# The last block's turning: eight units through the matrix engine, or through 32x32 blocks and memory

## The chip, the cores and the metric

One core of a Trainium2 chip runs the whole program. The metric is the device time of one execution in microseconds (us), lower is better. Engines are named as in the profile: PE is TensorE (PEld its weight loads), DVE VectorE, ACT ScalarE, POOL GpSimd, SP the queue that issues most transfers.

## The reference, cut to what matters

Two blocks of a network on 256 tokens of width 1024; the change lies in the second one, whose mixer is this (one layer, 16 heads of 64):

```python
proj = jnp.einsum("bsd,dc->bsc", h, w_in)                 # 1024 -> 10240 columns
xc, bg, cg, zc, q, k, v, za, g_conv, g_attn = jnp.split(proj, splits, axis=-1)
c = causal_depthwise_conv(cg * xc, conv_w)                # three taps along the tokens
y_conv = jnp.einsum("bsc,cd->bsd", jax.nn.silu(zc) * bg * c, w_out_conv)
o = mixture_of_dilations(q, k, v, slopes)                 # softmax attention, three patterns
y_attn = jnp.einsum("bsc,cd->bsd", jax.nn.silu(za) * o, w_out_attn)
merged = sigmoid(g_conv + b) * y_conv + sigmoid(g_attn + b) * y_attn
return jnp.einsum("bsd,de->bse", merged, w_o)
```

## The kernel before, in words

Tokens lie on partitions in two tiles of 128. All weights pass through a ring: SP loads a slot of 1 MB (two transfers of 512 KB, `load`, L483 to L500) into one of three raw buffers, ACT rounds it to the high part (`round_hi`, L675), POOL subtracts for the low part in four pieces (`subtract`, L642), and PE multiplies with high and low parts (`across_tile`, L2062, L2063, L2065: 24 matmuls of 512 columns for both token tiles). SP asks for the low part of the slot three back before it loads the next, ACT rounds four slots ahead of PE (`ahead`), and the split buffers are six.

`HI` is the input product of the last block: 40 slots, two for each of 20 column groups of 512, in the order q, q, k, k, v, v, then the inputs of the convolution (6 to 9), gates (10 to 15) and merge gates (16 to 19). Each engine's `hybrid` walks through the same loop over groups `c` and halves `j` and does its share of the other work between slots. From `c = 5` on, one `step(k)` per slot handles the heads: PE makes scores of two heads at each even step (L2604) and the value products of head k - 5 (L2620 to L2622); DVE adds the position bias (L1767), takes maxima (L1769, L1770), and for head k - 1 multiplies with the pattern table and sums (L1775, L1777) and turns the probabilities by 32x32 blocks (`v.transpose`, L1783); ACT exponentiates (L1104).

Two ways of turning stand side by side. The probabilities go through memory: after DVE's block transposes of a pair of heads, SP stores them in four transfers (L556), waits for these, and loads them in four more, in pieces of 128 bytes, to their turned place (L562); `turn_heads(m)` does this after the weight load of slot 19 + 2m. The other eight units, q (two), k (two), the convolution's input (7, 9) and the convolution's gate (11, 13), are turned by PE: `unit` (L2624) makes four transposes per token tile into one PSUM bank, and ACT copies them to SBUF (`units`, L1114); for 11 and 13 DVE multiplies them out of PSUM (`z_units`, L1831). The convolution itself (`convolve`, L1819 to L1821) is DVE's, eight pieces of 128 channels, three passes each.

The turned probabilities are the stationary operand of the value products, q that of the scores, k the moving operand of the scores. Waits are explicit semaphores, and each engine executes its instructions in the order written.

Of the kernel before, what the change touches and what calls it, by code (L numbers as in the profile page):

```python
# [23 lines left out]
F32 = mybir.dt.float32  # L24
F32R = mybir.dt.float32r
# [6 lines left out]
P = 128  # L32
# [107 lines left out]
def program(nc, A, out):  # L140
    ctx = ExitStack()
    with ctx:
# [14 lines left out]
        pT_hi = sb("pT_hi", [P, 2, TILES * P], F32R)  # L157
        pT_lo = sb("pT_lo", [P, 2, TILES * P], F32R)
# [3 lines left out]
        causal = sb("causal", [P, LCOLS])  # L162
        upto = sb("upto", [P, P])
        ones = sb("ones", [P, P])
        last_row = sb("last_row", [P, P])
# [16 lines left out]
        def area(at, *shape):  # L182
# [5 lines left out]
            if len(shape) == 3:  # L188
# [61 lines left out]
        h_bounce = [nc.dram_tensor(f"h_bounce{w}", (4, P, 2 * LCOLS // 4), F32, kind="Internal").ap()  # L250
# [10 lines left out]
        H_UNITS = {0: h_qT[:, 0:4], 1: h_qT[:, 4:8], 2: h_kT[:, 0:4], 3: h_kT[:, 4:8], 7: h_uT[:, 0:4],  # L261
                   9: h_uT[:, 4:8], 11: None, 13: None}
# [183 lines left out]
        h_pl_in_psum = sem("h_pl_in_psum")  # L446
        h_pl_ready = sem("h_pl_ready")
# [23 lines left out]
        def _(sp):  # L471
# [93 lines left out]
            def linear(s0, w, cols, halves_first=False, after={}):  # L565
# [5 lines left out]
                for i, (col, j) in enumerate(order):  # L571
# [4 lines left out]
                    if i in after:  # L576
                        turn_heads(after[i])

            def ple(name, w_proj, w_gate):
# [19 lines left out]
            linear(S["HI"], A["w_in_2"][0], [512 * c for c in H_ORDER],  # L599
                   after={H_TURN_SLOT + 2 * m: m for m in range(AH // 2)})  # L600
# [12 lines left out]
        def _(pool):  # L613
# [8 lines left out]
            pool.memset(causal[:], 0.0).then_inc(consts_ready, 1)  # L622
            pool.memset(upto[:], 1.0).then_inc(consts_ready, 1)
            pool.memset(ones[:], 1.0).then_inc(consts_ready, 1)
            pool.memset(last_row[:], 0.0).then_inc(consts_ready, 1)
# [6 lines left out]
            pool.affine_select(out=upto[:], in_=upto[:], compare_op=ALU.is_ge, fill=0.0, base=0,  # L632
                               pattern=[[1, P]], channel_multiplier=-1).then_inc(consts_ready, 1)
            pool.affine_select(out=last_row[:], in_=last_row[:], compare_op=ALU.not_equal, fill=1.0,
# [27 lines left out]
        def _(act):  # L662
# [214 lines left out]
            def p_hi(layer):  # L877
                act.wait_ge(pt_in_psum, layer + 1)
                nc.scalar.copy(pT_hi[:], (acc[:, 1, 0:512], tb[:, 1, :])[layer].rearrange("p (k c) -> p k c", k=2)
                               ).then_inc(pt_hi_ready, 1)  # L880
# [209 lines left out]
            def hybrid():  # L1090
# [17 lines left out]
                def units(c):  # L1108

                    dst = H_UNITS[c]  # L1110
# [1634 lines left out]
```

## Time and profile before

| | |
|---|---|
| median of 3 runs | 1367.21 us (1365.07 to 1367.71) |
| profiled execution | 1366.17 us, span 1364.4 us |
| granted clock of PE in it | 0.997 of full speed |
| busy in the span | PE 1348.8, PEld 1121.2, DVE 624.0, ACT 658.0, POOL 1140.3 us |
| moved by DMA | 255.36 MB, mean 187 GB/s |

The page gives busy times of the engines; matmul ends are modelled, so the spacing of starts tells more than the busy share. Windows give the same by stretch of time; the lists of waits tell which instruction stood idle for which other; the order of time shows single instructions. The input product of the last block takes the stretch from about 1040 to 1288 us, its middle 32 slots from 1063 to 1266.

### The profile page before, as it was taken

The numbers are of one execution on the slowest core, as the hardware profiler recorded it, in microseconds if no ns is written. First come the engines' busy times: TensorE is split into PE (matmuls) and PEld (weight loads), VectorE is DVE, ScalarE is ACT, GpSimd is POOL, SyncE is SP. The second block draws the span as 40 slices with busy tenths as digits, with TensorE's granted clock in tenths as the row PEclk, the third lists the DMA queues.
The fourth block names the chain that finished last, engine by engine and source line by source line (L and its number), as shares of the span: only waits on it lengthen the run. The fifth ranks groups of instructions, "written<-read, shape, count | busy, mean of one in ns | idle before, by whom it ended". The sixth has DMA issues, their size and how long they took to land.

```text
span 1364.4 us, 19630 instructions
## 1 busy us (share of the span) xinstructions
PE 1348.8 (99%) x6723; PEld 1121.2 (82%) x6723; DVE 624.0 (46%) x1570; ACT 658.0 (48%) x757; POOL 1140.3 (84%) x913
## 2 busy tenths in 40 slices
PE   8999999999999999999999999999999999999997
PEld 6888888888888888888888778888888888878886
DVE  6233344654333356623333885333346236862224
ACT  6444454546444456444443676444446443444431
POOL 5999977849999969999998539999978977779882
PEclk9999999999999999999999999999999999999999
DMA  8666654536666555766558426665545557767540
GB/s 273 215 201 208 206 183 144 185 106 225 197 192 194 194 171 171 237 210 211 184 184 217 139 77 208 210 198 187 184 154 196 192 193 202 215 183 256 190 165 31
DMA packets 199488, 255.36 MB, mean 187 GB/s; under 512 B 42844, under 2 KB 137860, under 8 KB 199300
## 3 DMA queue, kind: packets, MB, share of 16 engines
q1 hardware_dynamic: 197140, 247.82, 57.0%
q10 hardware_dynamic: 2288, 6.75, 1.4%
q8 instruction: 37, 0.61, 0.2%
q14 instruction: 23, 0.19, 0.0%
HBM read 249.29 MB, written 5.24 MB: 187 GB/s over the span
## 4 chain that ended last, share of the span: by engine, by line
PE 92%; DVE 4%; ACT 1%; DMA 1%; issue 1%; SPq 0%; ACTq 0%; DVEq 0%
PE tb L2152 9%; PE gu L2152 9%; PE acc L2062 8%; PE acc L2063 8%; PE acc L2065 7%; PE acc L2099 6%; PE acc L2102 6%; PE acc L2107 6%; PE gu L2062 5%; PE gu L2063 5%; PE tb L2158 4%; PE gu L2158 4%; PE gu L2065 3%; PE gu L2070 2%; PE tb L2065 1%; PE tb L2062 1%
## 5 line engine op out<-in xcount | busy, mean ns | idle before, releaser
L642 POOL TENSOR_TENSOR w_lo<-w_raw,w_hi 128x512 fp32r<-128x512 f32 x896 | 1135.3, 1315 | 197.1 <-ACT w_hi L675 193.7
L675 ACT CAST w_hi<-w_raw 128x2048 fp32r<-128x2048 f32 x225 | 427.8, 1909 | 146.1 <-DMA w_raw<-in_w_ffn_in 36.3
L2152 PE MATMUL gu<-xT,w_hi 128*128 128x512 f32 x512 | 202.3, 395 | 0.0
L2152 PE MATMUL tb<-xT,w_hi 128*128 128x512 f32 x512 | 202.2, 395 | 0.0
L2062 PE MATMUL acc<-w_hi,xT 128*128 128x512 f32 x496 | 198.3, 400 | 0.0
L2063 PE MATMUL acc<-w_lo,xT 128*128 128x512 f32 x496 | 193.1, 389 | 0.0
L2065 PE MATMUL acc<-w_hi,xT 128*128 128x512 f32 x468 | 182.7, 390 | 0.0
L1378 DVE TENSOR_TENSOR arena<-gu,arena 128x256 f32<-128x256 f32 x64 | 27.2, 425 | 300.5 <-PE gu L2152 300.5
L2158 PE MATMUL tb<-xT,w_lo 128*128 128x256 f32 x512 | 140.4, 280 | 0.0
L2158 PE MATMUL gu<-xT,w_lo 128*128 128x256 f32 x512 | 139.8, 279 | 0.0
L2062 PE MATMUL gu<-w_hi,xT 128*128 128x512 f32 x312 | 123.4, 395 | 1.1 <-ACT xT L720 1.1
L2063 PE MATMUL gu<-w_lo,xT 128*128 128x512 f32 x312 | 121.4, 389 | 0.0
L2158 PEld LDWEIGHTS tb<-xT,w_lo 128*128 128x128 f32 x512 | 96.4, 188 | 20.2
L2158 PEld LDWEIGHTS gu<-xT,w_lo 128*128 128x128 f32 x512 | 96.2, 188 | 19.1
L2062 PEld LDWEIGHTS acc<-w_hi,xT 128*128 128x128 f32 x496 | 93.2, 188 | 18.9 <-issue 1.2
L2063 PEld LDWEIGHTS acc<-w_lo,xT 128*128 128x128 f32 x496 | 93.3, 188 | 18.2 <-issue 0.2
L2099 PE MATMUL acc<-w_hi,hidden_T 128*128 128x512 f32 x336 | 104.4, 392 | 0.0
L2102 PE MATMUL acc<-w_lo,hidden_T 128*128 128x512 f32 x336 | 103.6, 390 | 0.0
L2107 PE MATMUL acc<-w_hi,hidden_T 128*128 128x512 f32 x336 | 103.5, 389 | 0.0
L2065 PEld LDWEIGHTS acc<-w_hi,xT 128*128 128x128 f32 x468 | 87.8, 188 | 18.9
L866 ACT ACTIVATE arena<-gu 128x256 f32<-128x256 f32 x32 | 12.3, 384 | 182.0 <-DVE gu L1381 182.0
L2152 PEld LDWEIGHTS tb<-xT,w_hi 128*128 128x128 f32 x512 | 97.1, 190 | 2.6
(364 smaller groups left out, 1969.0 us busy)
## 6 DMA issues: line engine op xcount, KB each, us to landing
w_raw<-in_w_ffn_in SPq DMA_DIRECT2D x176, 512.0 KB, 4.7
w_raw<-in_w_ffn_out SPq DMA_DIRECT2D x88, 512.0 KB, 4.1
w_raw<-in_w_in SPq DMA_DIRECT2D x80, 512.0 KB, 4.6
w_raw<-in_mlstm_w_in SPq DMA_DIRECT2D x24, 512.0 KB, 4.3
w_raw<-in_w_ple_gate SPq DMA_DIRECT2D x16, 512.0 KB, 4.1
w_raw<-in_w_kv SPq DMA_DIRECT2D x16, 512.0 KB, 4.3
w_raw<-in_mlstm_w_out SPq DMA_DIRECT2D x8, 512.0 KB, 4.5
w_raw<-in_diff_w_q SPq DMA_DIRECT2D x8, 512.0 KB, 5.2
```

The costliest lines, as they stand in the source:

```text
L642: ins = pool.tensor_tensor(w_lo[:, slot.spl, cols], w_raw[:, slot.raw, cols], w_hi[:, slot.spl, cols].bitcast(F32), ALU.subtract)
L675: nc.scalar.copy(w_hi[:, slot.spl, :], w_raw[:, slot.raw, :]).then_inc(hi_ready, 1)
L1378: v.tensor_tensor(part, low, rs_row, ALU.mult).then_inc(row_step, 1)
L2062: mm(out, xh, wh, start=(half == 0 and k == 0), stop=False)
L2063: mm(out, xh, wl, start=False, stop=False)
L2065: last = mm(out, xl, wh, start=False, stop=(half == 1 and k == 3))
L2070: last = mm(out, xl, wh, start=False, stop=(half == 1 and k == 3))
L2099: mm(acc[:, t, 512 * half:512 * half + 512], a_hi[:, k, tok(t)], w(w_hi, half), start=st, stop=False)
L2102: mm(acc[:, t, 512 * half:512 * half + 512], a_hi[:, k, tok(t)], w(w_lo, half), start=False, stop=False)
L2107: last = mm(acc[:, t, 512 * half:512 * half + 512], a_lo[:, k, tok(t)], w(w_hi, half), start=False, stop=sp_)
L2152: return mm(pair_of(j), w_hi[:, slot.spl, at:at + P], xT[:, 4 * half + k, :, :].rearrange("p a c -> p (a c)"), start=(half == 0 and k == 0 ...
L2158: return mm(pair_of(j)[:, 0:2 * P], w_lo[:, slot.spl, at:at + P], xT_hi[:, 4 * half + k, :], start=False, stop=False)
```

## The change

PE's transposes of the eight units, ACT's copies and the PSUM bank between them go. DVE turns each unit by 32x32 blocks right behind its evacuation (`turn_unit`), SP stores it to memory in four transfers that put the blocks to their turned partitions, and loads it back in one. q and k come back as before (channel block, then token). The convolution's input and gate come back token by token, with the four channel blocks side by side (a step of 16 bytes from token to token); the probabilities likewise with their six blocks (a step of 24 bytes from query to query), in one transfer of 3 KB per partition in place of four with pieces of 128 bytes. A second buffer of blocks for the heads is laid over tables that are no longer used. Storing and loading of a pair of heads stand behind the weight loads of different slots. The convolution's pieces come one to two slots later, its gate is multiplied at groups 15 and 17 in one pass over both token tiles, and the merge bias is loaded in two halves.

```diff
-H_CONVOLVE = {(9, 0): 0, (9, 1): 1, (10, 0): 2, (10, 1): 3, (11, 0): 4, (12, 0): 5, (12, 1): 6, (13, 0): 7}
-H_UNITS_AT = {(2, 0): 0, (2, 1): 1, (3, 0): 2, (4, 0): 3, (8, 1): 7, (10, 1): 9, (12, 1): 11, (14, 1): 13}
+H_CONVOLVE = {(10, 0): 0, (10, 1): 1, (11, 0): 2, (11, 1): 3, (13, 0): 4, (13, 1): 5, (14, 0): 6, (14, 1): 7}
+H_GATE_AT = {(15, 0): 11, (17, 0): 13}
+H_UNITS = (0, 1, 2, 3, 7, 9, 11, 13)
+H_BLOCKS_FREE = {7: 3, 9: 7, 11: 0, 13: 11}
+H_STORE_UNITS = {10: (0, 1), 12: (2,), 14: (3,), 22: (7,), 27: (9,), 31: (11,), 34: (13,)}
+H_LOAD_UNITS = {11: (0, 1), 13: (2,), 15: (3,), 23: (7,), 28: (9,), 32: (11,), 35: (13,)}
...
-        h_uT = area(8192, 8, 256)
+        h_uT = area(8192, 2, 256, 4)
-        h_pb = area(13056, 4, 2 * 3 * 32)
+        h_pb = [area(13056, 4, 2 * 3 * 32), tables[:].rearrange("p a b -> p (a b)").rearrange("p (j n) -> p j n", j=4)]
-            "p (w i n) -> p w i n", w=2, i=6)
+            "p (w c n) -> p w c n", w=2, n=6)
...
-            def turn_heads(m):
+            def scatter_blocks(bounce, blocks, stored):
+                pieces = bounce.rearrange("(b j) (n i a) -> b (j n) i a", j=4, i=4, a=32)
+                for i in range(4):
+                    sp.dma_start(pieces[:, :, i, :],
+                                 blocks[32 * i:32 * i + 32].rearrange("b j (n a) -> b (j n) a", a=32)
+                                 ).then_inc(stored, 16)
+            def scatter_runs(bounce, blocks, n, stored):
+                pieces = bounce.rearrange("(b j) (t i r) -> b (j t) i r", j=4, i=4, r=32 * n)
...
+            def store_heads(m):
                 sp.wait_ge(h_blocks_turned, 2 * m + 2)
-                if m:
-                    sp.wait_ge(h_pt_landed, 64 * m)
-                for i in range(4):
-                    sp.dma_start(h_bounce[m % 2][i].rearrange("(j b) n -> b j n", j=4), h_pb[32 * i:32 * i + 32]
-                                 ).then_inc(h_bounced, 16)
+                scatter_runs(h_bounce[m % 2], h_pb[m % 2], 6, h_bounced)
+            def load_heads(m):
                 if m >= 2:
                     sp.wait_ge(h_pv_in_psum, 2 * m - 2)
+                if m:
+                    sp.wait_ge(h_pt_landed, 16 * m)
                 sp.wait_ge(h_bounced, 64 * (m + 1))
-                for i in range(4):
-                    sp.dma_start(h_pT[:, m % 2, :, 32 * i:32 * i + 32],
-                                 h_bounce[m % 2][i].rearrange("c (n a) -> c n a", a=32)).then_inc(h_pt_landed, 16)
+                sp.dma_start(h_pT[:, m % 2].rearrange("p c n -> p (c n)"), h_bounce[m % 2]).then_inc(h_pt_landed, 16)
+            def store_unit(c):
+                sp.wait_ge(h_unit_turned, H_UNIT_NO[c] + 2)
...
+            def load_unit(c):
+                n = H_UNITS.index(c)
+                sp.wait_ge(h_unit_stored, 128 if n < 2 else 64 * (n + 1))
+                if n:
+                    sp.wait_ge(h_unit_landed, 16 * n)
+                sp.dma_start(h_turned[c].rearrange("p k c -> p (k c)"), h_unit_bounce[c]).then_inc(h_unit_landed, 16)
+            def turns_after(i):
+                m = i - H_TURN_SLOT
+                if m >= 0 and m % 2 == 0 and m // 2 < AH // 2:
+                    store_heads(m // 2)
+                if m >= 1 and m % 2 == 1 and m // 2 < AH // 2 - 1:
+                    load_heads(m // 2)
+                if m == AH - 2:
+                    load_heads(AH // 2 - 1)
+                for c in H_LOAD_UNITS.get(i, ()):
+                    load_unit(c)
+                for c in H_STORE_UNITS.get(i, ()):
+                    store_unit(c)
...
-                        if h >= 2 and h % 2 == 0:
-                            dve.wait_ge(h_bounced, 64 * (h // 2))
-                        to = h_pb[:, :, 96 * (h % 2):96 * (h % 2) + 96].rearrange("p j (n a) -> p n j a", n=3)
-                        v.transpose(to, s.rearrange("p (n j b) -> p n j b", n=3, j=4)).then_inc(h_blocks_turned, 1)
+                        if h >= 4 and h % 2 == 0:
+                            dve.wait_ge(h_bounced, 64 * (h // 2 - 1))
+                        to = h_pb[(h // 2) % 2].rearrange("p j (a n) -> p n j a", n=6)[:, 3 * (h % 2):3 * (h % 2) + 3]
+                        v.transpose(to, s.rearrange("p (n b j) -> p n j b", n=3, j=4)).then_inc(h_blocks_turned, 1)
...
+                def turn_unit(c):
+                    if c in H_BLOCKS_FREE:
+                        dve.wait_ge(h_unit_stored, 64 * (H_UNITS.index(H_BLOCKS_FREE[c]) + 1))
+                    for t in range(TILES):
+                        dve.wait_ge(h_evac, H_EVAC[c] - 1 + t)
+                        if c < 4:
+                            to = h_blocks[c].rearrange("p j (k t a) -> p t k j a", t=TILES, a=32)[:, t]
+                        else:
+                            to = h_blocks[c].rearrange("p j (t a k) -> p t k j a", t=TILES, a=32)[:, t]
+                        v.transpose(to, h_s[:, H_PLACE[c], t, :].rearrange("p (k b j) -> p k j b", j=4, b=32)
+                                    ).then_inc(h_unit_turned, 1)
...
+                    z = h_zT[:, 4 * half:4 * half + 4, :]
+                    v.tensor_tensor(z, h_turned[c].rearrange("p c k -> p k c"), z, ALU.mult).then_inc(h_z_ready, 2)
...
-                            return h_pT[:, (h // 2) % 2, 3 * (h % 2) + n, :]
+                            return h_pT[:, (h // 2) % 2, :, 3 * (h % 2) + n]
...
-                def unit(c, t):
-                    pe.wait_ge(h_evac, H_EVAC[c])
...
-                    for k in range(4):
-                        ins = nc.tensor.transpose(tb[:, 1, tok(k)], h_s[:, H_PLACE[c], t, tok(k)], ident[:])
-                    ins.then_inc(h_pl_in_psum, 1)
```

## Rows read from the trace of the kernel before

**Rows 1.** The page, part 1: busy us (share of span) and instructions by engine.

```profile
PE 1348.8 (99%) x6723; PEld 1121.2 (82%) x6723; DVE 624.0 (46%) x1570; ACT 658.0 (48%) x757; POOL 1140.3 (84%) x913
```

**Rows 2.** Windows: busy us of PE, PEld, DVE, ACT, POOL; clock, DMA share, GB/s.

```profile
1157.00:1184.00 27.00, 26.78 (x138) 21.76 (x136) 21.82 (x54) 14.12 (x18) 17.15 (x15) 1.00 0.74 214
1184.00:1206.00 22.00, 21.29 (x112) 16.81 (x110) 19.15 (x39) 8.90 (x10) 19.29 (x15) 1.00 0.75 217
```

**Rows 3.** All waits of PE, 1063 to 1266 us: total, times, longest.

```profile
PE tb L2634 <- DVE arena L1831: 0.9, 1, 0.9
PE tb L2634 <- ACT arena L1114: 0.2, 1, 0.2
```

**Rows 4.** PE in order of time around one unit's transposes: start, duration.

```profile
1065.62 0.39 PE L2063 MATMUL acc<-w_lo,xT 128*128 128x512 f32 x1
1065.85 0.39 PE L2065 MATMUL acc<-w_hi,xT 128*128 128x512 f32 x1
1066.08 0.60 PE L2634 MATMUL tb<-ident,arena 128*128 128x128 f32 x4
1066.43 0.47 PE L2062 MATMUL acc<-w_hi,xT 128*128 128x512 f32 x1
1066.74 0.39 PE L2063 MATMUL acc<-w_lo,xT 128*128 128x512 f32 x1
```

**Rows 5.** PE in order of time around the transposes that waited longest.

```profile
1204.90 0.39 PE L2065 MATMUL acc<-w_hi,xT 128*128 128x512 f32 x1
1206.19 0.63 PE L2634 MATMUL tb<-ident,arena 128*128 128x128 f32 x4 [0.90 <-DVE arena L1831]
```

**Rows 6.** PE in order of time around the first value product.

```profile
1135.40 0.39 PE L2065 MATMUL acc<-w_hi,xT 128*128 128x512 f32 x1
...
1135.63 0.33 PE L2620 MATMUL gu<-arena,hidden_T 128*128 128x64 f32 x2
...
1136.21 0.48 PE L2062 MATMUL acc<-w_hi,xT 128*128 128x512 f32 x1
```

**Rows 7.** Groups of instructions, 1063 to 1266 us: busy, mean ns | idle before, releaser.

```profile
L642 POOL TENSOR_TENSOR w_lo<-w_raw,w_hi 128x512 fp32r<-128x512 f32 x133 | 170.7, 1324 | 34.4 <-ACT w_hi L675 34.4
...
L2634 PE MATMUL tb<-ident,arena 128*128 128x128 f32 x64 | 9.6, 272 | 1.1 <-DVE arena L1831 0.9 <-ACT arena L1114 0.2
L1783 DVE STREAM_TRANSPOSE arena<-arena 128x384 f32<-128x384 f32 x16 | 9.1, 567 | 15.0 <-DMA h_bounce<-arena 15.0
```

**Rows 8.** DVE, then POOL, in order of time, 1158 to 1170 us.

```profile
1158.43 0.42 DVE L1777 CUSTOM_DVE_ANT_0 arena<-arena,times 128x256 f32<-128x256 f32 x1
...
1162.40 1.50 DVE L1777 CUSTOM_DVE_ANT_0 arena<-arena,times 128x256 f32<-128x256 f32 x1
...
1161.02 9.06 POOL L642 TENSOR_TENSOR w_lo<-w_raw,w_hi 128x512 fp32r<-128x512 f32 x7 [2.74 <-ACT w_hi L675]
```

**Rows 9.** Groups of DVE's instructions, 540 to 580 us (another stage).

```profile
L1986 DVE TENSOR_TENSOR arena<-arena,gcol 128x1024 f32<-128x1024 f32 x2 | 4.6, 2325 | 0.0
...
L1979 DVE STREAM_TRANSPOSE arena<-arena 128x1024 f32<-128x1024 f32 x2 | 2.4, 1224 | 0.0
```

**Rows 10.** PE, POOL and SP's queue in order of time: the first pair.

```profile
1117.22 0.93 PE L2604 MATMUL gu<-arena 64*128 64x128 f32 x8
...
1122.11 10.27 POOL L642 TENSOR_TENSOR w_lo<-w_raw,w_hi 128x512 fp32r<-128x512 f32 x8 [1.92 <-ACT w_hi L675]
...
1126.73 2.63 SPq L562 DMA_DIRECT2D hidden_T<-h_bounce  x4
```

**Rows 11.** Transfers issued from 1063 to 1266 us: KB each, median us to landing.

```profile
w_raw<-in_w_in SPq DMA_DIRECT2D x62, 512.0 KB, 4.6
h_bounce<-arena SPq DMA_DIRECT2D x32, 96.0 KB, 4.3
hidden_T<-h_bounce SPq DMA_DIRECT2D x32, 96.0 KB, 2.8
...
arena<-in_b_merge ACTq DMA_DIRECT2D x1, 1024.0 KB, 4.5
```

More of the change, by code:

```diff
@@ L161, in program @@
         ident = sb("ident", [P, P])
[L162 to L165, printed above, removed]
+        tables = sb("tables", [P, 6, P])
+        causal = tables[:, 0:3].rearrange("p a b -> p (a b)")
+        upto, ones, last_row = (tables[:, i] for i in (3, 4, 5))
         gcol = sb("gcol", [P, 168])
@@ new lines, in scatter_runs @@
+            def scatter_runs(bounce, blocks, n, stored):
+                pieces = bounce.rearrange("(b j) (t i r) -> b (j t) i r", j=4, i=4, r=32 * n)
+                for i in range(4):
+                    sp.dma_start(pieces[:, :, i, :],
+                                 blocks[32 * i:32 * i + 32].rearrange("b j (t r) -> b (j t) r", r=32 * n)
+                                 ).then_inc(stored, 16)
+            def store_heads(m):
+                sp.wait_ge(h_blocks_turned, 2 * m + 2)
+                scatter_runs(h_bounce[m % 2], h_pb[m % 2], 6, h_bounced)
@@ L567, in linear @@
+            def linear(s0, w, cols, halves_first=False, after=None):
                 src = w.rearrange("(k p) c -> p k c", p=P)
@@ L575, in linear @@
                                  src[:, 4 * j + 2 * k:4 * j + 2 * k + 2, col:col + 512]) for k in range(2)])
-                    if i in after:
-                        turn_heads(after[i])
+                    if after:
+                        after(i)
             def ple(name, w_proj, w_gate):
@@ L598, in _ @@
             ple("P1", A["w_ple_proj"][1], A["w_ple_gate"][1])
-            linear(S["HI"], A["w_in_2"][0], [512 * c for c in H_ORDER],
-                   after={H_TURN_SLOT + 2 * m: m for m in range(AH // 2)})
+            linear(S["HI"], A["w_in_2"][0], [512 * c for c in H_ORDER], after=turns_after)
             linear(S["HC"], A["w_out_conv_2"][0], both)
@@ L878, in p_hi @@
                 act.wait_ge(pt_in_psum, layer + 1)
-                nc.scalar.copy(pT_hi[:], (acc[:, 1, 0:512], tb[:, 1, :])[layer].rearrange("p (k c) -> p k c", k=2)
+                nc.scalar.copy(pT_hi, (acc[:, 1, 0:512], tb[:, 1, :])[layer].rearrange("p (k c) -> p k c", k=2)
                                ).then_inc(pt_hi_ready, 1)
@@ L1106, in step @@
                         ins.then_inc(h_exped, 1)
-                def units(c):
-                    dst = H_UNITS[c]
-                    for t in range(TILES):
-                        w = H_UNIT_NO[c] + t
-                        act.wait_ge(h_pl_in_psum, w + 1)
-                        nc.scalar.copy(dst[:, :, tok(t)], tb[:, 1, :].rearrange("p (k c) -> p k c", k=4)
-                                       ).then_inc(h_pl_ready, 1)
                 steps = 0
@@ L1121, in hybrid @@
                             ahead(At(s0 + 2 * c + j))
-                        if H_UNITS.get(H_UNITS_AT.get((c, j))) is not None:
-                            units(H_UNITS_AT[c, j])
                         if c >= 5 and steps < H_STEPS:
@@ L1822, in convolve, with gate_conv @@
                                            ).then_inc(h_conv, 1)
-                def z_units(c):
+                def gate_conv(c):
                     half = (c - 11) // 2
                     dve.wait_ge(h_conv, 4 * half + 4)
-                    for t in range(TILES):
-                        dve.wait_ge(h_pl_in_psum, H_UNIT_NO[c] + t + 1)
-                        z = h_zT[:, 4 * half:4 * half + 4, tok(t)]
-                        v.tensor_tensor(z, tb[:, 1, :].rearrange("p (k c) -> p k c", k=4), z, ALU.mult
-                                        ).then_inc(h_z_ready, 1)
+                    dve.wait_ge(h_unit_landed, 16 * (H_UNITS.index(c) + 1))
+                    z = h_zT[:, 4 * half:4 * half + 4, :]
+                    v.tensor_tensor(z, h_turned[c].rearrange("p c k -> p k c"), z, ALU.mult).then_inc(h_z_ready, 2)
                 def gate_before_sigmoid(c, t):
-                    dve.wait_ge(h_bm_landed, 16)
+                    dve.wait_ge(h_bm_landed, 16 if c < 18 else 32)
                     dve.wait_ge((tile0_used, slot_used)[t], s0 + 2 * c + 2)
                     g = (h_gc, h_ga)[c // 18][:, t, 512 * (c % 2):512 * (c % 2) + 512]
-                    v.scalar_tensor_tensor(g, bank(c, t), r(t), h_bm[:, 512 * (c - 16):512 * (c - 16) + 512],
+                    v.scalar_tensor_tensor(g, bank(c, t), r(t), h_bm[:, 512 * ((c - 14) % 4):512 * ((c - 14) % 4) + 512],
                                            ALU.mult, ALU.add).then_inc(h_gpre, 1)
@@ L1844, in hybrid @@
                     for j in range(2):
-                        if H_UNITS_AT.get((c, j)) in (11, 13):
-                            z_units(c - 1)
                         if c >= 5 and steps < H_STEPS:
@@ L2329, in cumulate @@
                     pe.wait_ge(m_logf, 1)
-                    mm(tb[:, 1, 16:24], upto[:], m_lf, start=True, stop=True).then_inc(m_cum, 1)
+                    mm(tb[:, 1, 16:24], upto, m_lf, start=True, stop=True).then_inc(m_cum, 1)
                 chunk(2, {0: turn_gates, 3: cumulate})
@@ L2337, in spread @@
                         pe.wait_ge(m_am_ready, t)
[L2338 removed]
+                    mm(tb[:, 0, :], ones, m_diag, start=True, stop=True).then_inc(m_spread, 1)
                 chunk(3, {0: lambda: spread(0)})
                 pe.wait_ge(m_last_rhs, 1)
[L2343 removed]
+                mm(tb[:, 1, 24:32], last_row, m_last, start=True, stop=True).then_inc(m_last_in_psum, 1)
                 spread(1)
@@ L2647, in hybrid @@
                             across_tile(At(s0 + 2 * c + j), j, t, acc_outs(c % 2, t))
-                            if (c, j) in H_UNITS_AT:
-                                unit(H_UNITS_AT[c, j], t)
                         if c >= 5 and steps < H_STEPS:
```

72 lines of the change are left out of this document (42 added, 30 removed).

## The prediction

> **What bounds the kernel now.** I read the page's busy times first: TensorE (PE) is busy 1348.8 of 1364.4 us [rows 1]. A busy PE row cannot tell a full engine from one that stretches, so I went on to the windows of the stage that the change touches, the 40 weight slots of the last block's input product, about 1063 to 1266 us. In its two densest windows PE is busy in 26.78 of 27 and 22.00 of 22 us, VectorE (DVE) in 21.82 and 19.15, GpSimd (POOL) in 17.15 and 19.29, ScalarE (ACT) in 14.12 and 8.90 [rows 2]. PE is the bound, DVE is second. PE's own waits in the whole stage come to 1.1 us, both in front of the transposes that the change removes, one for DVE's gate product and one for ACT's copy [rows 3]. The third view is the order of time on PE: matmuls of 512 columns follow each other every 0.23 us (1065.62, 1065.85) [rows 4]. A slot is 24 of them, 5.5 us, and whatever else stands in PE's queue is added to the end of the kernel.
>
> **What is removed from PE.** Eight units of two token tiles are turned by PE, four transposes each, 64 in all [rows 7]. From the last matmul before such a four (1065.85) to the first behind it (1066.43) it is 0.58 us, and that first one takes 0.31 to the next: over two beats of 0.23 that is 0.43 us [rows 4]. I take 0.44, and 16 x 0.44 = **7.0 us** go. With them go the two waits. One is seen directly: the last matmul starts at 1204.90 and the transposes at 1206.19, 1.29 us for a beat of 0.23 [rows 5], so 1.06; the other is 0.2 [rows 3]. Together **1.3 us**. Nothing moves in between to take their place at once, since the next work in the queue, values of a head or the next slot, asks for things that are ready. PE's sum is -8.3 us.
>
> **What is added to PE.** No instruction. But the 48 value products now load their probabilities with 24 bytes between neighbouring columns (six blocks side by side) instead of 4. Before, a head's six loads and products take 1135.40 to 1136.21, 0.81 us less a beat, plus the 0.08 behind: 0.66, or 0.11 us a pass [rows 6]. The product has only 64 columns, so the pass is paced by its weight load of 128 columns, and a slower load is seen in full. No load in the trace has such a step. Bounds: 0, or a load of twice the time, 96 x 0.11 = 10.6 us. I take 0: the load draws 128 columns in 0.11 us, 0.86 ns each, whereas the same memory feeds moving columns at 0.23 us for 512, 0.45 ns each [rows 4, 6], so the load asks for half the pace that is proven. That is an argument for spare speed in contiguous order, not a measurement of steps, and the upper end stays in the range.
>
> The Trainium skill speaks against this layout: Advanced Engine Details and Errata, section SBUF Cachelines, says that SBUF lines are 16 bytes, that two hits on a line are needed to absorb the memory's latency, and that a new line at each access costs. By it each column at 24 bytes is a new line and the 10.6 us would come. It gives no size, and no row of the trace of before has such an access. It is the first rival below.
>
> **What is added to DVE.** 16 transposes of 128x512. The key transposes elsewhere in the kernel take 1.224 us for 128x1024 and the head transposes 0.567 for 128x384 [rows 7, 9], so 0.61 to 0.76 each, 10 to 12 us in all. The four gate products of 0.69 from PSUM become two of 128x1024 out of SBUF, 2.325 us each by the nearest row [rows 9], +1.9. What goes is DVE's wait for the bounce buffer, 15.0 us [rows 7], because it is doubled. Transposes, convolution and gate also get steps of 16 and 24 bytes; as above 0, upper end a doubling (16 x 0.57 for the heads, 16 x 0.6 for the units, some 0.5 for each of 24 convolution passes: 31 us, spread over 150). All of this lies beside PE's slots. The cover is this: at each step PE's value product waits for the row maxima of a head whose scores were issued a slot, 5.5 us and more, earlier. DVE's cost of a step depends on POOL: the same 128x256 pass takes 0.42 us when POOL is idle and 1.50 when it works (POOL is idle for 2.74 us up to 1161.02 and busy behind it) [rows 8]. With POOL working, I make a step 4.2 us and a convolution 3.5. The four slots of the convolutions 0 to 3 then ask 31 us of DVE with their 2.9 us of evacuation and unit transposes, against 4 x 6.6 on PE with its head work. It falls 5 us behind, which is just the cover. I charge 1.0 us.
>
> **What moves on the queues.** SP issued 64 transfers for the heads; now it issues 40 for them and 40 for the units, between the same weight loads. Where it waits, weight loads wait behind it, then ACT's rounding and POOL's subtraction. POOL finishes slots 17 and 18 at 1132.4, so slot 17 about 1127.3, while PE, which ends slot 15 at 1135.6, cannot reach it before 1141.7 [rows 6, 10]: a lead of 14 us. A unit holds SP for four issues (about 0.45 each), a store (4.3) and a load's issue [rows 11], some 7 us. The lead covers that; without it the loss would be 7 us less what is left. Bytes: the 8 units add 0.5 MB out and in each; of pieces of 128 bytes 16,400 come (units 0 to 3, 128 x 32 each) and 24,600 go (8 pairs, 128 x 24). Weights land in 4.6 us now [rows 11], and 2 us more on some of them is covered as well. Units 0 to 2 are needed at the end of slot 10, unit 2 is evacuated after slot 5, 27 us before, and its own chain (DVE 2.7, store 4.3 to 9, load 4.6) takes 12 to 16: nothing.
>
> The new wait that could tell is the probabilities'. SP used to stay for the bounce and to load the pair at once; now the load goes behind the next slot's weights, which wait for POOL's low part three slots back. For the first pair: scores start at 1117.22 and end at 1118.1, POOL has slot 17 at 1127.3, then two weight issues (0.9) and the pair's load, between 2.8 on its own and 4.6 + 2.8 one after the other [rows 10, 11]: 1131 to 1135.6. PE asks at 1135.6 [rows 6]. Later pairs have about 2 us more, for value products then stand between. Before, the same load was issued at 1126.73 [rows 10]. So a stall of 0 to 1 us for the first and little for others; with a DVE that is behind, its lag adds to this chain. I charge 0.5 us.
>
> **ACT and POOL.** ACT loses 12 copies, with the waits in front of them. It is not the bound, so 0; its rounding comes a little earlier, which helps the chain above. The merge bias is loaded in two halves; the second is issued behind ACT's sigmoids of slot 35 and lands some 4.5 us later [rows 11]. DVE asks for it after slot 37's first tile, and PE then still has six half slots, 6 x 12 x 0.23 = 16.6 us, before it needs what DVE makes of it: 0. POOL: 33 slots of 4 x 1.324 are 171 us of 203 [rows 7]; with 195 it still fits.
>
> **Sum**, against the profiled execution's 1366.17 us (span 1364.4): -7.0 - 1.3 + 1.0 + 0.5 = -6.8, 1359.4. The median of the runs shown, 1367.21, stands 1.0 above that execution; I predict **1359.6**.
>
> **The rivals.**
> (a) *The strided weight loads are slow.* Place: the 96 loads of the value products. Price up to +10.6; it decides from a pass of 0.20 us on, because then 96 x 0.09 eats the 8.3. At twice the time, with 1.5 for DVE and the queue, 1366.2 - 8.3 + 10.6 + 1.5 = 1370.0, **slower**; DVE's passes at half speed would add stalls and make it 1372. For it: the layout is new to the trace, and the pass is paced by the load. Against: the spare pace above. Chance 0.25.
> (b) *The wait moves to the probabilities.* DVE falls behind and the pair's load lies behind weights, so PE stalls at most of the 8 pairs by 0.5 to 1 us beyond my 1.5. For it: DVE is busy 41 of 49 us in the dense windows [rows 2], and the slack of 0 to 4 us is worked out from single landings. Against: 15.0 us of waiting leave DVE [rows 7], and SP no longer stays for the bounce. Time 1362 to 1367, say 1364.5. Chance 0.2.
> (c) *The time does not change because something else paces PE.* If POOL's 5.3 us a slot ruled, PE's removed work would turn into waits for low parts. Against: POOL idles 34.4 us in the stage for want of ACT's rounding [rows 7], and PE never waits for it [rows 3]. Time 1366. Chance 0.05.
> My forecast, 0.5: 1357.5 to 1361.5.
>
> **How the numbers follow.** About 0.2%, 2.7 us, is what a measurement of this kernel can tell from no change, so faster means below 1364.5, slower above 1369.9. Faster: 0.5 and half of (b), 0.1, with a little of (a) where the loads are only half as slow again (1364): 0.62. Slower: two thirds of (a), 0.17. The rest is the same, 0.21. The range starts at 1357.0, all of 8.3 gained with a run 1 us below the profiled one, and reaches over (b) and (c) into (a) to 1370.0, with about 0.15 beyond it.
>
> **What would show it.** In the profile after, no transposes between the matmuls of this stage: the spacing is 0.23 throughout with gaps only at scores and values. The six passes of a value product span 0.58 us over a beat as before; 1.2 would be (a). PE's waits: if the load of the probabilities from the bounce, or DVE's maxima, stand in front of PE with over 4 us in total, it is (b); waits for low parts would be (c). DVE's unit transposes take 0.6 to 0.8 us; if 1.2, steps cost DVE. The prediction is wrong if the end comes less than 4 us earlier, or if more than 9 us go, which no row of PE's queue could supply.

## The result, and the profile after

The change makes the kernel slower: 1372.47 us in the median (1370.88 to 1373.20) against 1367.23 us before (1365.07 to 1367.88), a ratio of 1.0039 with a 95% interval of [1.0029, 1.0048]. A seventh execution took 1917.47 us at a granted clock of 0.654 and is left out of the range and the ratio. The profiled execution took 1372.22 us, its span is 1370.5 us; before they were 1366.17 and 1364.4.

PE's transposes of units are gone from the stage and its busy time rose all the same. The page of the changed kernel, part 1, answers to [rows 1]:

```profile
PE 1352.1 (99%) x6659; PEld 1125.6 (82%) x6659; DVE 658.5 (48%) x1584; ACT 651.6 (48%) x745; POOL 1146.7 (84%) x913
```

64 instructions fewer and 3.3 us more: something on PE got longer. The order of time on PE shows what. First a value product that waits for nothing, the counterpart of [rows 6]:

```profile
1151.97 0.40 PE L2126 MATMUL acc<-w_hi,xT 128*128 128x512 f32 x1
1152.21 0.44 PE L2683 MATMUL gu<-arena,hidden_T 128*128 128x64 f32 x2
1152.49 0.61 PE L2684 MATMUL gu<-arena,hidden_T 128*128 128x64 f32 x2
1152.93 0.61 PE L2685 MATMUL gu<-arena,hidden_T 128*128 128x64 f32 x2
1153.35 0.47 PE L2123 MATMUL acc<-w_hi,xT 128*128 128x512 f32 x1
```

From the last matmul before it to the first behind it are 1.38 us, before 0.81 [rows 6]. Two passes are 0.44 us apart (1152.49, 1152.93): 0.22 us a pass, twice the 0.11 of before. That is 0.57 us a head, for 16 heads 9.1 us, more than the 8.3 that the prediction takes off PE.

The second loss stands at the first pair of heads, in the order of time on PE of the changed kernel:

```profile
1131.67 0.39 PE L2126 MATMUL acc<-w_hi,xT 128*128 128x512 f32 x1
1134.91 0.71 PE L2683 MATMUL gu<-arena,hidden_T 128*128 128x64 f32 x2 [2.85 <-DMA hidden_T<-h_bounce]
1135.41 0.65 PE L2684 MATMUL gu<-arena,hidden_T 128*128 128x64 f32 x2
1135.86 0.65 PE L2685 MATMUL gu<-arena,hidden_T 128*128 128x64 f32 x2
1136.27 0.77 PE L2123 MATMUL acc<-w_hi,xT 128*128 128x512 f32 x1
...
1141.54 0.46 PE L2123 MATMUL acc<-w_hi,xT 128*128 128x512 f32 x1
```

PE starts 3.24 us after the last matmul, 3.0 more than a beat, because the probabilities are not there. Behind the wait the next 12 matmuls take 5.27 us (1136.27 to 1141.54), where 12 beats of 0.227 are 2.72: another 2.55 us. The windows of the changed kernel say why (columns as in [rows 2]):

```profile
1131.00:1136.30 5.30, 2.45 (x12) 1.95 (x10) 4.20 (x10) 2.70 (x3) 5.30 (x5) 0.86 0.78 265
1136.30:1141.50 5.20, 5.20 (x13) 4.08 (x14) 3.68 (x5) 0.00 (x0) 5.20 (x5) 0.50 0.90 282
1157.00:1184.00 27.00, 27.00 (x129) 22.39 (x128) 20.62 (x48) 10.54 (x14) 18.43 (x15) 1.00 0.74 224
```

PE stood idle for 2.85 us, and then the granted clock is 0.50, the 1.2 GHz level, for the whole next window; PE counts as busy all the while. Later the clock is full again, and PE has no gap.

Why the probabilities are late is seen in SP's queue of the changed kernel (start, time over which the issues of one line go on, count):

```profile
1069.13 8.37 SPq L565 DMA_DIRECT2D h_unit<-arena  x8
...
1080.00 6.00 SPq L605 DMA_DIRECT2D arena<-h_unit  x2
1086.05 0.94 SPq L510 DMA_DIRECT2D w_raw<-in_w_in  x2
1087.04 6.11 SPq L565 DMA_DIRECT2D h_unit<-arena  x4
...
1097.48 7.20 SPq L565 DMA_DIRECT2D h_unit<-arena  x4
...
1124.75 2.72 SPq L573 DMA_DIRECT2D h_bounce<-arena  x4
...
1130.16 0.34 SPq L589 DMA_DIRECT2D hidden_T<-h_bounce  x1
```

The stores of units 0 to 3 go out in pieces of 128 bytes, and four such transfers hold SP for 4 to 7 us (L565). The loads of the first two units hold it as well (1080.00, 6.00 us): the second is issued only when the first has landed, and SP stands for 5.3 us of that time. What SP issues after them, the weights and then the pair's blocks, is late, and the pair is loaded at 1130.16 against 1126.73 before [rows 10]. Meanwhile PE is early: its first value product could have started at 1131.9, not at the 1135.6 of before [rows 6].

DVE and POOL do more. Groups of the changed kernel, 1063 to 1272 us, against [rows 7, 9]:

```profile
L697 POOL TENSOR_TENSOR w_lo<-w_raw,w_hi 128x512 fp32r<-128x512 f32 x131 | 175.1, 1374 | 35.8 <-ACT w_hi L730 35.8
L1851 DVE STREAM_TRANSPOSE arena<-arena 128x512 f32<-128x512 f32 x14 | 14.8, 1102 | 0.0
...
L1831 DVE STREAM_TRANSPOSE tables<-arena 128x384 f32<-128x384 f32 x8 | 7.5, 937 | 0.0
```

DVE's wait for the bounce buffer (15.0 us) is gone, the unit transposes take 1.10 us, those of the heads 0.93 where they took 0.567. PE waits for neither DVE nor POOL: all its waits in the changed kernel, 1063 to 1272 us (total, times, longest; [rows 3] before), are

```profile
PE gu L2683 <- DMA hidden_T<-h_bounce: 2.8, 1, 2.8
```

The account against the span of before: value products +9.1, wait for the first pair +3.0, low clock +2.55, together +14.7; the span grew by 6.1, so the removed transposes and their waits gave 8.6. That is a remainder, but it can also be read directly. Where four transposes stood in [rows 4], between 1065.85 and 1066.43, the order of time on PE of the changed kernel now has

```profile
1065.78 0.39 PE L2126 MATMUL acc<-w_hi,xT 128*128 128x512 f32 x1
1066.00 0.39 PE L2123 MATMUL acc<-w_hi,xT 128*128 128x512 f32 x1
```

The 16 such places, compared matmul by matmul in the two profiles, give 8.5 us: 0.45 at each, and 1.3 of waits. Ahead of the stage and behind it the two kernels run alike, to within 0.1 us.

### The profile page after: what moved, and what is told of

It reads as the page before. It is cut to its first block, busy times and chain, and to the rows that moved or that the text cites. A ratio compares the mean times of both kernels' runs of the same rounds, so it can differ in the third digit from the quotient of the medians.

```text
span 1370.5 us, 19512 instructions
## 1 busy us (share of the span) xinstructions
PE 1352.1 (99%) x6659; PEld 1125.6 (82%) x6659; DVE 658.5 (48%) x1584; ACT 651.6 (48%) x745; POOL 1146.7 (84%) x913
## 4 chain that ended last, share of the span: by engine, by line
POOL 62%; issue 18%; PE 17%; DMA 2%; DVE 1%; ACT 0%; SPq 0%; POOLq 0%; ACTq 0%; DVEq 0%
POOL w_lo L697 62%; PE acc L2123 4%; PE acc L2126 4%; PE acc L2124 4%; DMA w_raw<-in_w_ffn_in 1%; PE tb L2126 1%; PE tb L2124 1%; PE tb L2123 1%; PE gu L2126 1%; PE gu L2123 1%; PE gu L2124 1%; PE gu L2684 1%; PE gu L2685 1%; PE gu L2683 0%; DMA hidden_T<-h_bounce 0%
## 5 line engine op out<-in xcount | busy, mean ns | idle before, releaser
L2213 PEld LDWEIGHTS gu<-xT,w_hi 128*128 128x128 f32 x512 | 96.3, 188 | 2.8 <-DVE hidden_T L1444 0.4
```

What stands on the lines that cost most here:

```text
L2213: return mm(pair_of(j), w_hi[:, slot.spl, at:at + P], xT[:, 4 * half + k, :, :].rearrange("p a c -> p (a c)"), start=(half == 0 and k == 0 ...
```

## The experiments

**1. The store a slot earlier.** The change with the heads' blocks stored and loaded one slot earlier.

```diff
-H_TURN_SLOT = 19
+H_TURN_SLOT = 18
```

> The changed kernel with one number changed: each pair of heads is stored behind the weights of the slot before (18 + 2m in place of 19 + 2m) and loaded behind 19 + 2m. Theory: of the 14 to 15 us that the change adds, 9.5 are value products whose passes take 0.22 us in place of 0.11, and 5.8 are one event, PE's 3.2 us of waiting for the first pair and the 2.6 us that half the clock costs behind it; 8.6 go with PE's transposes. Then the wait and the low clock go here, the passes stay at 0.22, and the time is 1366.5 (1365 to 1368). Rival, the stall is the new pace of SP's queue and comes back at a later pair: 1370 to 1373. Rival, the half clock has nothing to do with the stall: PE still runs some 6.8 us at 0.5 somewhere in this stage, 1369.

Measured 1367.15 us, ratio 1.0001 [0.9992, 1.0010]. All waits of PE in this kernel, 1063 to 1266 us (total, times, longest):

```profile
PE gu L2667 <- DMA arena<-h_unit: 0.6, 1, 0.6
```

No wait for the pair is left, the clock stays at 1.00 through the stage, the passes stay at 0.22. The wait and the low clock cost 5.3 us (1372.47 - 1367.15), close to the 3.0 + 2.55 of the account; without them the change moves nothing, for about 9 us went and 9 us came.

**2. Packed probabilities.** The change with the probabilities in packed blocks as before (four transfers in, four out), at the places of the change.

```diff
-            "p (w c n) -> p w c n", w=2, n=6)
+            "p (w i n) -> p w i n", w=2, i=6)
...
-                            return h_pT[:, (h // 2) % 2, :, 3 * (h % 2) + n]
+                            return h_pT[:, (h // 2) % 2, 3 * (h % 2) + n, :]
```

> The changed kernel with the heads' part alone undone: probabilities packed again (128 neighbouring columns, loaded in four transfers in pieces of 128 bytes), stored and loaded behind the same slots as in the change; the eight units stay with DVE and memory. Theory, the 24-byte step of the stationary operand doubles its load: the six passes are back at 0.11 us each, the stall of the first pair and the half clock behind it stay or shrink, and the time is 1363 (1359 to 1364). Rival, the passes are slow for another reason (transfers that run at the same time, more of them than before): they stay at 0.2 and the time stays at 1372.

Measured 1368.82 us, ratio 1.0018 [1.0008, 1.0028]: 5 to 6 us above what was expected. The passes did go back to 0.11. The order of time on PE in this kernel, at the first pair, shows the miss:

```profile
1132.15 0.39 PE L2130 MATMUL acc<-w_hi,xT 128*128 128x512 f32 x1
1137.04 0.69 PE L2687 MATMUL gu<-arena,hidden_T 128*128 128x64 f32 x2 [4.50 <-DMA hidden_T<-h_bounce]
1137.52 0.63 PE L2688 MATMUL gu<-arena,hidden_T 128*128 128x64 f32 x2
1137.95 0.63 PE L2689 MATMUL gu<-arena,hidden_T 128*128 128x64 f32 x2
```

The wait grew to 4.7 us over a beat instead of staying at 3.0, and two later pairs waited as well (6.9 us in three waits). At the first pair PE asks no sooner than in the changed kernel (1132.15 against 1131.67). What is longer is the issue of the load: four transfers in pieces of 128 bytes take 3.89 us from 1130.54 on, one transfer took 0.34 us at 1130.16. The granted clock then falls to 0.50 here too. Curing one loss made the other larger: the two parts have to be undone together.

**3. Both.** Packed probabilities and the store a slot earlier.

> Both at once: packed probabilities and the store one slot earlier. Theory: 1367.2 - 8.6 = 1358.6, at best 1357, with no wait of PE over 0.5 us from slot 4 to 36 and no low clock; faster than both kernels. Rival, DVE or SP's queue holds PE up once it is faster: 1361 to 1366, with waits of PE for maxima, for probabilities or for low parts.

Median 1362.88 us, ratio 0.9982 [0.9966, 0.9998], but the 12 times lie in two groups: eight from 1360.72 to 1363.85 and four from 1369.27 to 1371.37. The profiled execution, 1369.79, belongs to the upper group. No value product waits in it. The lower group lies 2 to 5 us above the 1358.6 that was expected, in the range of the rival, and the profile has a wait of its kind: 1.9 us for a low part of POOL's in the last slots. The larger loss is in three orders of time of this kernel, of PE, DVE and POOL:

```profile
1281.93 0.39 PE L2130 MATMUL acc<-w_hi,xT 128*128 128x512 f32 x1
1288.93 0.76 PE L2127 MATMUL gu<-w_hi,xT 128*128 128x512 f32 x1 [6.61 <-DVE xT L1937]
...
1275.14 14.24 DVE L1937 TENSOR_TENSOR xT<-arena,xT 128x512 fp32r<-128x512 f32 x2
...
1290.63 1.28 DVE L1937 TENSOR_TENSOR xT<-arena,xT 128x512 fp32r<-128x512 f32 x2
...
1254.63 33.61 POOL L701 TENSOR_TENSOR w_lo<-w_raw,w_hi 128x512 fp32r<-128x512 f32 x27
```

Two subtractions of DVE that take 1.28 us a little later took 14.24 us. POOL worked from 1254.63 to 1288.24 without a pause, and DVE was through at 1289.38. PE, which needs these low parts for the next projection, lost 6.8 us, and its granted clock was 0.50 for the next 5 us, which cost some 2.5 more. The two groups are about 8.4 us apart.

**4. The step by itself.** The stationary operand of the value products is read at steps of 1, 2, 3, 4, 5 and 6 columns, by heads; the store is a slot earlier, and other probabilities than the reference's are multiplied.

```diff
+                            g = (1, 1, 1, 2, 2, 2, 3, 3, 3, 4, 4, 4, 5, 5, 6, 6)[h]
```

> The store one slot earlier, and the stationary operand of the value products is read with another step in each group of heads, from the same landed buffer: 1 column for heads 0 to 2, 2 for 3 to 5, 3 for 6 to 8, 4 for 9 to 11, 5 for 12 and 13, 6 for 14 and 15 (4, 8, 12, 16, 20, 24 bytes). It multiplies with wrong probabilities. One profile gives the pass for each step. Theory by 16-byte lines that want two hits: 0.11 us at 4 and 8 bytes, something between at 12, 0.22 from 16 on. Rival, any step but 4 bytes doubles the load: 0.22 from 8 on. Rival, it is not the step: the same at all.

The order of time on PE in this kernel; two rows a head, two passes apart, at steps of 4, 8, 12, 16 and 24 bytes:

```profile
1132.85 0.39 PE L2686 MATMUL gu<-arena,hidden_T 128*128 128x64 f32 x2
1133.07 0.39 PE L2687 MATMUL gu<-arena,hidden_T 128*128 128x64 f32 x2
...
1159.62 0.40 PE L2686 MATMUL gu<-arena,hidden_T 128*128 128x64 f32 x2
1159.85 0.40 PE L2687 MATMUL gu<-arena,hidden_T 128*128 128x64 f32 x2
...
1173.11 0.51 PE L2686 MATMUL gu<-arena,hidden_T 128*128 128x64 f32 x2
1173.45 0.51 PE L2687 MATMUL gu<-arena,hidden_T 128*128 128x64 f32 x2
...
1201.56 0.63 PE L2686 MATMUL gu<-arena,hidden_T 128*128 128x64 f32 x2
1202.02 0.63 PE L2687 MATMUL gu<-arena,hidden_T 128*128 128x64 f32 x2
...
1228.50 0.61 PE L2686 MATMUL gu<-arena,hidden_T 128*128 128x64 f32 x2
1228.94 0.61 PE L2687 MATMUL gu<-arena,hidden_T 128*128 128x64 f32 x2
```

A pass takes 0.11, 0.115, 0.17, 0.23 and 0.22 us. The step is free up to 8 bytes, the price rises between, and it is flat from 16 bytes on. The kernel's transfers are those of experiment 1, and the pass follows the step from head to head, so it is the step and not the traffic that sets it. That is the rule of the Trainium skill, Advanced Engine Details and Errata, section SBUF Cachelines: lines of 16 bytes, two hits a line needed. At 8 bytes a line is hit twice, at 16 once. The Trainium skill gives no size; here it is 0.11 us for a load of 128 columns. With that line length, steps of 8, 12 and 16 bytes touch 64, 96 and 128 lines, and an estimate from the three passes is 1.8 ns a line in each case.

**5. The step alone.** The kernel before with only the heads' probabilities side by side (one load of 3 KB pieces, step of 24 bytes).

> The kernel before with one part of the change alone: the probabilities of a pair are stored in runs and loaded token by token with six blocks side by side (one load, a step of 24 bytes in the stationary operand); the units are still turned by TensorE and the blocks of a pair stored at the kernel before's places. Theory (the step alone costs 0.11 us per pass of four matmuls, 0.55 to 0.66 us per head, some 9.5 us in all, and nothing covers it, since TensorE is the bound here): value products alone 1.14 us over the beat instead of 0.585, with scores 2.30 instead of 1.64, time 1367.2 + 9.5 = 1376.7 us (1375 to 1378). Rival (the step is partly paid out of waits that the kernel before has anyway, or the single load with 3 KB pieces brings something back): 1367 to 1373 us.

Measured 1377.29 us, ratio 1.0078 [1.0063, 1.0092]: +10.1 us against the expected 9.5. The step is paid in full and nothing of it comes back. Not all of the 10.1 need be the step: in the profiled execution the longest wait in front of the transposes grew from 0.9 to 1.5 us, with 3.4 us at half clock behind it.

**6. The pieces of the units' stores.** The change with units 0 to 3 stored in pieces of 512 bytes; their blocks then come in another order, so the scores are of other numbers, at the same amount of work.

```diff
-                if c < 4:
-                    scatter_blocks(h_unit_bounce[c], h_blocks[c], h_unit_stored)
-                else:
-                    scatter_runs(h_unit_bounce[c], h_blocks[c], 4, h_unit_stored)
+                scatter_runs(h_unit_bounce[c], h_blocks[c], 4, h_unit_stored)
```

> The changed kernel with the units of the queries and keys stored in pieces of 512 bytes, like the other units, instead of 128 bytes; the four units then reach TensorE with their blocks in another order, so that the scores are of other numbers, and the work and its amount are the same. Theory (the stores of these four units in small pieces hold SyncE's queue, so that the weights of slots 11 to 15 are issued 4 to 9.5 us later and the first pair's probabilities 3.4 us later, which costs the wait of 3.2 us and 2.6 us at half clock behind it): the weights of slot 12 issued by about 1081 us instead of 1086, the first pair's wait under 1 us, no low clock behind it, time 1372.4 - 5.8 = 1366.6 us (1365.5 to 1368). Rival (the size of the pieces does not matter, the eight transfers and their place in the queue do): wait and time as with the change, 1371 to 1373 us.

Median 1367.76 us, ratio 1.0017 [1.0005, 1.0029], the profiled execution 1366.19. SP's queue in this kernel:

```profile
1082.50 0.94 SPq L510 DMA_DIRECT2D w_raw<-in_w_in  x2
1083.49 2.87 SPq L573 DMA_DIRECT2D h_unit<-arena  x4
...
1124.39 0.47 SPq L589 DMA_DIRECT2D hidden_T<-h_bounce  x1
```

A unit of four transfers holds SP for 2.9 us instead of 6 to 7, the weights of slot 12 go out at 1082.50 instead of 1086.05, and the pair is loaded 5.8 us earlier. PE has no wait left in the stage. So in this execution it is the small pieces of units 0 to 3 that made the first pair late, not the number of transfers. Four of the ten times lie at 1370.6 to 1372.4, where the changed kernel lies; none of them was profiled, and what parts them from the others stays open.

**7. The merge bias earlier.** Experiment 3, with the second half of the merge bias loaded before the sigmoids of groups 16 and 17, since DVE had waited for it until 1273.8 us.

> The change with packed probabilities and the store a slot earlier, and the second half of the merge bias loaded before the sigmoids of chunks 16 and 17 instead of after the rounding of the two next slots (the load's issue stood 17 us behind the gate that frees its place, 1268.70 against 1251.04). Theory A (the low parts for the next projection begin late, at 1275.1 us, since VectorE waits for that bias until 1273.8 us; begun at about 1271.6 us they end in time): no group of slow times, median 1361.5 us (1360.5 to 1363). Theory B (VectorE's subtraction of two operands in SBUF does not get going while GpSimd works without a pause, whenever it begins; in the profiled run it took 13.64 us, until 0.55 us after GpSimd's pause): times still come in two groups, some at 1361 and some at 1367 to 1371 us; in a profile of the second group a subtraction of 128x512 takes over 5 us.

Measured 1371.47 us, ratio 1.0038 [1.0025, 1.0051]: all five times in the upper group. DVE, then POOL, in order of time in this kernel:

```profile
1273.00 16.55 DVE L1938 TENSOR_TENSOR xT<-arena,xT 128x512 fp32r<-128x512 f32 x2 [0.56 <-ACT xT L1205]
...
1253.48 34.91 POOL L701 TENSOR_TENSOR w_lo<-w_raw,w_hi 128x512 fp32r<-128x512 f32 x28
```

Begun 2.1 us earlier, the two subtractions took 2.3 us longer and ended just as late: 1.2 us after POOL's pause at 1288.39. Theory A falls. The hold ends with POOL's pause, here and in experiment 3, as theory B has it.

**8. A pause.** Experiment 7, and ACT rounds no further slot until DVE has the first tile's low parts, so that POOL runs out of work.

```diff
                     if t == 0:
+                        act.wait_ge(t_lo_ready, 4 * T["HC"] + 2)
                         ahead(At(s0 + 38))
```

> The kernel of the early bias, and ScalarE rounds no further slot until VectorE has both low parts of the first token tile, so that GpSimd runs out of work for a moment. Theory B (VectorE's subtraction is held for as long as GpSimd's stream has no pause): one group of times only, median 1361.5 us (1360.5 to 1363), the subtraction over within 2 us of GpSimd's last instruction; GpSimd loses up to 3 us there, and its lead over TensorE (11 us at that place) covers it. Theory A (only the late bias mattered): the same times as the early bias alone. Rival C (the slow times come from another place, for instance the heads' loads): two groups of times here too.

Measured 1363.73 us (1360.86 to 1365.86), ratio 0.9976 [0.9966, 0.9985]: one group of times, faster than both kernels, 2.2 us above what was expected. DVE, then POOL, in order of time in this kernel:

```profile
1274.08 7.26 DVE L1939 TENSOR_TENSOR xT<-arena,xT 128x512 fp32r<-128x512 f32 x2
...
1253.97 26.23 POOL L701 TENSOR_TENSOR w_lo<-w_raw,w_hi 128x512 fp32r<-128x512 f32 x21
```

POOL now stops at 1280.20 and DVE is through at 1281.34. ACT stood still for 6.89 us up to 1281.38, so it is not ACT that held DVE. PE waited 4.4 us for low parts of POOL's, against 1.9 in the profile of experiment 3; that is the size of the 2.2 us. POOL had no lead left at the end of the stage. Its order of time says where the lead went:

```profile
1230.04 16.03 POOL L701 TENSOR_TENSOR w_lo<-w_raw,w_hi 128x512 fp32r<-128x512 f32 x10 [6.43 <-ACT w_hi L734]
```

It idled for 6.43 us, since SP stayed for the landing of the last pair's store before it issued the weights of slot 33.

**9. The last pair like the others.** Experiment 8, and the last pair is loaded after the next slot's weights.

```diff
-                if m >= 1 and m % 2 == 1 and m // 2 < AH // 2 - 1:
+                if m >= 1 and m % 2 == 1 and m // 2 < AH // 2:
                     load_heads(m // 2)
-                if m == AH - 2:
-                    load_heads(AH // 2 - 1)
```

> The kernel with the pause, and the last pair's probabilities loaded after the next slot's weights, like those of the other pairs (the change loads them in the same place where it stores them, so SyncE stays for the store's landing: in the kernel with the pause from 1213.1 to 1218.4 us, the weights of slot 33 are issued at 1221.8, GpSimd idles 6.4 us up to 1230.0, and its lead over TensorE falls from 12.5 to 3.9 us and to nothing at slots 37 to 39). Theory (that one wait in SyncE's queue is where GpSimd's lead goes; the probabilities come no later, for the store needs its 5 us anyway): GpSimd's lead stays above 6 us to slot 39, TensorE waits for no low part there, and the 4.4 us of such waits and about 1.5 us of low clock behind them go: 1363.7 - 4 to 5 = 1359.3 us (1358 to 1361). Rival (GpSimd lags because its pieces are longer beside VectorE's work, 6 to 7.6 us a slot, and will lag anyway): 1362.5 to 1365 us, the waits for low parts stay.

Measured 1359.66 us (1358.67 to 1360.23), ratio 0.9949 [0.9936, 0.9962]: the fastest kernel without an upper group, 7.5 us under the kernel before. All waits of PE in it, 1063 to 1266 us:

```profile
PE gu L2671 <- DMA arena<-h_unit: 0.4, 1, 0.4
PE gu L2687 <- DMA hidden_T<-h_bounce: 0.3, 1, 0.3
```

The waits for low parts in the stage are gone, as expected, though POOL's lead did shrink to 1.2 us at slot 39, not the 6 that was forecast: in this the rival was right. The hold is shorter here and not gone: the first subtraction takes 5.68 us, until POOL's pause, and is over before PE needs it.

**10. Without the pause.** Experiment 3 with the last pair of experiment 9 alone.

> Packed probabilities, store a slot earlier, and the last pair loaded after the next slot's weights; no early bias, no pause for GpSimd. Theory (GpSimd works without a pause at the end of the stage only because it has lost its lead there; with the lead it waits for free places between slots, as in the kernel before, and VectorE's subtraction gets in): one group of times at 1359.5 us (1358 to 1361.5), the first subtraction under 4 us in the profile. Rival (the subtraction is held whenever its start falls between two of GpSimd's instructions, lead or no lead): two groups again, some at 1366 to 1370 us.

Median 1361.46 us, ratio 0.9966 [0.9947, 0.9985], but 12 times from 1357.32 to 1368.56, six of them over 1364. The profiled one, 1357.97, has no hold and no wait of PE in the stage. DVE, then POOL, in order of time in it:

```profile
1269.91 2.90 DVE L1935 TENSOR_TENSOR xT<-arena,xT 128x512 fp32r<-128x512 f32 x2
...
1229.07 63.34 POOL L699 TENSOR_TENSOR w_lo<-w_raw,w_hi 128x512 fp32r<-128x512 f32 x45 [0.30 <-ACT w_hi L732]
```

POOL makes no pause here, and DVE got its two subtractions in all the same. So the theory, that the lead gives POOL pauses, is wrong, and the times come in two groups as the rival said. The lead makes the fast outcome faster, by some 4 us; one group of times is seen only with the pause (experiments 8 and 9, 15 executions). That the executions over 1364 are held as in experiment 3 is not shown, for none of them was profiled.

## Why the prediction was wrong

The forecast was 1359.6 us, the time 1372.5, beyond the range's 1370. By the prediction's own steps:

- *Removed from PE, -8.3.* Right: 8.5 read directly, 8.6 by the account. Experiment 10, which keeps this part and removes the losses, has a profiled execution of 1357.97, 8.2 us under the one before; experiment 9 ends 7.5 us under the kernel before with 0.7 us of waits left in the stage and 1.0 behind it.
- *Strided weight loads, "I take 0".* **The first step that failed.** It measured 9.1 us in the profile after and 10.1 alone (experiment 5, with the longer wait there), next to the upper bound of 10.6. The argument was that a load asks for half the pace that moving columns prove [rows 4, 6]. But that pace was proven for neighbouring columns, and it says nothing of columns that lie 24 bytes apart. Experiment 4 shows that the spare pace existed (8 bytes are free) and was used up at 16 bytes. The rule that the prediction quotes against the layout was the better evidence. Rival (a) was the mechanism, at a chance of 0.25; its 1370.0 lacked the wait below.
- *DVE, +1.0.* Not seen: PE waits for DVE nowhere in the stage. (The prediction's 31 us of DVE are the four steps and four convolutions alone; with the 2.9 us that it names they are 33.7.) The bound was needed all the same: with the 24-byte step the heads' transposes take 0.93 us, and in the packed kernels 0.558.
- *SP's queue, "the lead covers that", and the first pair at +0.5.* **The second step that failed.** The lead of 14 us did cover PE's need of weights; PE waited for no low part. But the pair's load stands in the same queue, and I dated it by POOL's times in the kernel before [rows 10], without the hold of units 0 to 3. The prediction did give each unit some 7 us of SP, mostly for a store's landing, and weighed them against the weights alone; measured, the issues by themselves took 6.1 and 7.2 us for a unit of four. Experiment 6 shows that this hold was it: with short holds the load goes out at 1124.4 instead of 1130.2. And I dated PE's demand by the kernel before too (1135.6), although the prediction itself takes eight unit tiles, 3.5 us, out of PE's queue ahead of it; PE asked at 1131.9. A wait of 0 to 1 us became 3.0. Rival (b) had the place right and the reason wrong: PE waited at one pair and not at most of them, and DVE was not behind.
- *No term for the clock.* The sum has none, and the wait was followed by 2.55 us at half clock. The waits of before were 0.9 us and less [rows 3], and no row read before showed what a longer one brings.
- *ACT and POOL, 0.* Right for the changed kernel. Rival (c), POOL, came true only where the other losses were removed: then POOL's lead ran out (experiment 8) and its unbroken stream held DVE (experiments 3, 7).

The sum with the measured terms: 1366.2 - 8.6 + 9.1 + 3.0 + 2.55 = 1372.25; it meets the profiled 1372.22 by construction, for the 8.6 is its remainder. What shows its terms independently are the 8.5 read from the two orders of time and experiments 1 (5.3 for 5.55) and 5 (10.1 for 9.1). One slip of the prediction decides nothing: 1359.4 and the 1.0 that it names make 1360.4, not 1359.6.

## What to carry to other kernels

Keep neighbouring columns of PE's stationary operand within 8 bytes of each other, or count a short pass at its full price: here a layout that saved three of four transfers cost 0.11 us in each of 96 loads. When work is taken off the bounding engine, date every demand anew, and date each transfer with all that now stands ahead of it in its queue, above all stores in small pieces. When the bounding engine speeds up, look at what the next engines share: here a stream of POOL's without a pause could hold DVE for 14 us and more.

## What the runs showed of the hardware

- A strided stationary load is not paced by PE's clock. In the changed kernel two passes took 0.45 us at the low clock (1135.41 to 1135.86) and 0.44 at the full one (1152.49 to 1152.93); two packed passes of experiment 2 took 0.43 us at the low clock (1137.52 to 1137.95) and 0.22 at the full one (1152.74 to 1152.96).
- A wait of some 3 us on PE cost nearly as much again afterwards: the granted clock fell to 0.50, and 12 matmuls took 5.27 us.
- A DVE subtraction with both operands in SBUF can be held through many of POOL's instructions in a row. In experiment 7 the two subtractions took 16.55 us, and POOL's pieces 1.25 us each (34.91 us for 28), so DVE was passed over about a dozen times in a row. The Trainium skill, SBUF — State Buffer, section SBUF: two separate sides, says of the port pair that both engines share that it is locked for a whole instruction and that the other engine blocks. The trace agrees in that DVE waits while POOL works, and goes further, for one instruction of POOL's would be 1.25 us. In other executions DVE got in without a pause of POOL's (experiment 10, 2.90 us for both); what decides that is not settled.
- Steps cost DVE as well: a transpose of 128x384 into a 24-byte step took 0.93 us against 0.558 packed.
